# Sums over features by products with 128 moving columns, and tile 0 of a transition finished first, in a streaming-encoder trunk

## The reference, cut to what matters

```
for i in range(DEPTH):                      # DEPTH = 2
    h = modulate(rms_norm(x, norm_g[i, 0]), sh_t, sc_t)
    h = s5_mixer(...) if i % 2 == 0 else diff_attention(...)
    x = x + g_t[:, None, :] * rms_norm(h, norm_g[i, 1])
    h = modulate(rms_norm(x, norm_g[i, 2]), sh_c, sc_c)
    h = conv_ffn(h, ...)
    x = x + g_c[:, None, :] * rms_norm(h, norm_g[i, 3])
```

## Time and profile before

| what | value |
|---|---|
| time, median of 3 runs | 1262.13 us (1261.72 to 1264.94) |
| profiled execution, span from the first to the last instruction | 1260.0 us |
| PE (TensorE matmul) busy | 1216.8 us, 97% |
| DVE (VectorE) busy | 765.5 us, 61% |
| ACT (ScalarE) busy | 527.6 us, 42% |
| POOL (GpSimd) busy | 382.8 us, 30% |
| mean granted TensorE clock | 0.983 |

### The profile page before, as it was taken

One profiled execution on the slowest core, in us unless ns is written; L12 is line 12 of the kernel. 1 busy time (PEld: TensorE's weight loads), 2 busy tenths in 40 slices (PEclk: granted clock), 3 DMA queues, 4 the chain that ended last, 5 costly groups with the idle time before them and its releaser, 6 DMA issues.

```text
span 1260.0 us, 17591 instructions
## 1 busy us (share of the span) xinstructions
PE 1216.8 (97%) x6439; PEld 977.3 (78%) x6439; DVE 765.5 (61%) x1077; ACT 527.6 (42%) x809; POOL 382.8 (30%) x261
## 2 busy tenths in 40 slices
PE   5978999999999999999999999999999999999997
PEld 2757888778888887888788777678788888887886
DVE  7989587888965543242873678858744444442225
ACT  3383454244434343141432577756444443441311
POOL 4970100244654333000212443510344434331000
PEclk9989999899999999999899999998999999999999
DMA  9857645246743123223123232311132222223221
GB/s 360 305 182 210 243 159 202 98 167 225 289 165 121 67 100 125 102 93 115 46 101 117 70 99 83 90 45 67 40 127 100 85 86 96 100 100 127 83 91 67
DMA packets 26696, 162.19 MB, mean 129 GB/s; under 512 B 4496, under 2 KB 4816, under 8 KB 8400
## 3 DMA queue, kind: packets, MB, share of 16 engines
q1 hardware_dynamic: 25632, 161.15, 36.4%
q10 hardware_dynamic: 1008, 0.28, 0.1%
HBM read 152.76 MB, written 2.10 MB: 123 GB/s over the span
## 4 chain that ended last, share of the span: by engine, by line
PE 85%; DVE 8%; issue 2%; ACT 2%; DMA 1%; SPq 1%; ACTq 0%; DVEq 0%; POOL 0%
PE psum L1887 17%; PE psum L1889 17%; PE psum L1888 17%; PE psum L2001 3%; PE psum L2094 3%; PE psum L2003 3%; PE psum L2095 3%; PE psum L2096 3%; PE psum L2002 3%; PE psum L1763 2%; PE psum L2151 1%; PE psum L1952 1%; PE psum L1726 1%; PE psum L2137 1%; PE psum L2139 1%
## 5 line engine op out<-in xcount | busy, mean ns | idle before, releaser
L1887 PE MATMUL psum<-hhi,whi 128*128 128x512 f32 x960 | 378.0, 394 | 1.0 <-DVE wlo L1280 0.5
L1889 PE MATMUL psum<-hhi,wlo 128*128 128x512 f32 x960 | 374.2, 390 | 0.0
L1888 PE MATMUL psum<-hlo,whi 128*128 128x512 f32 x960 | 373.9, 389 | 0.0
L1280 DVE TENSOR_TENSOR wlo<-raw,whi 128x2048 fp32r<-128x2048 f32 x81 | 193.5, 2388 | 176.2 <-ACT whi L716 176.2
L716 ACT ACTIVATE whi<-raw 128x2048 fp32r<-128x2048 f32 x80 | 153.1, 1914 | 165.4 <-PE psum L2096 76.4
L1887 PEld LDWEIGHTS psum<-hhi,whi 128*128 128x128 f32 x960 | 180.6, 188 | 43.0 <-issue 3.5
L559 POOL TENSOR_TENSOR ca<-ca,cb 128x512 f32<-128x512 f32 x44 | 139.4, 3168 | 236.4 <-ACT ca L841 236.4
L1889 PEld LDWEIGHTS psum<-hhi,wlo 128*128 128x128 f32 x960 | 180.3, 188 | 38.1
L1888 PEld LDWEIGHTS psum<-hlo,whi 128*128 128x128 f32 x960 | 180.4, 188 | 36.0
L1445 DVE SCALAR_TENSOR_TENSOR ca<-psum,convp,ca 128x511 f32<-128x511 f32 x44 | 32.9, 748 | 204.1 <-ACT ca L837 204.1
L843 ACT ACTIVATE ghi<-ca 128x512 f32 (+1 forms) x44 | 27.8, 632 | 152.2 <-POOL ca L559 152.2
(11 more groups left out here) (366 smaller groups left out, 1854.5 us busy)
## 6 DMA issues: line engine op xcount, KB each, us to landing
raw<-in_units SPq DMA_DIRECT2D x92, 1024.0 KB, 4.8
ada_raw<-in_ada_w SPq DMA_DIRECT2D x24, 1024.0 KB, 7.4
ada_ring<-in_ada_w SPq DMA_DIRECT2D x24, 1024.0 KB, 4.8
qk_sw<-ca SPq DMA_DIRECT2D x32, 128.0 KB, 2.3
u<-in_x_blocks SPq DMA_DIRECT2D x1, 2048.0 KB, 10.4
x<-in_x_t SPq DMA_DIRECT2D x1, 2048.0 KB, 9.6
out_rows<-y_late SPq DMA_DIRECT2D x8, 256.0 KB, 2.1
bc_par<-in_s_bc SPq DMA_DIRECT2D x1, 1024.0 KB, 5.8
```

The lines of the kernel that those rows point to most:

```text
L1280: TT(wlo[:, s, :], raw[:, s, :], whi[:, s, :].bitcast(F32), ALU.subtract).then_inc(split_lo, 1)
L1887: M(out, w_hi, hi[:, k, :], start=(k == 0), stop=False)
L1888: M(out, w_hi, lo[:, k, :], start=False, stop=False)
L1889: return M(out, w_lo, hi[:, k, :], start=False, stop=(k == KT - 1))
```

## The change

All three sums now use 128 moving columns. For B the moving operand is the tile of ones. For A and C it is a table `ac_w` whose two columns are repeated 64 times: A wants weight 1 and C the squared gate, so one product of y's square gives both A (first column) and C (second column). Tiles that are summed in this way ("direct") need no second square on ScalarE and no additions for A and C on VectorE: tiles 6 and 7 in transitions 0 and 1, and all eight in transition 2, where six of them are put between the products of the last unit before the transition. The last tile's product x*g*y is no longer added to `cb[:, 0]`; TensorE takes it in from `bx`. In transition 0 it is computed from the ungated tile. The division by 1024 goes into the roots.

In `next_input` tile 0 is finished (line 1429 then 1417) before tiles 1 and 2 are gated, and `low(f)` stands behind tile f in place of tile f-1. The idle products are moved: none stands before or between the sums now, and after them 12, 5, 11 (6+2, 2, 11 in transition 2) in place of 4, 7, 14.

```diff
-        DIRECT_A, DIRECT_C = ((7,), (7,), (6, 7)), ((), (), (6, 7))
+        DIRECT = ((6, 7), (6, 7), tuple(range(KT)))
+        W_A, W_C = 3 * KT, 3 * KT + 1
...
+        def square_of(r, f):
+            if r == 2:
+                return (sq[:, 0, :], sq[:, 1, :], ca[:, 0, :], ca[:, 1, :])[f % 4]
+            return sq[:, f % 2, :] if f else ssum[:]
...
+            nc.gpsimd.memset(ac_w[:, 0:W_C, 0], 1.0).then_inc(const_ready, 1)
+            nc.gpsimd.memset(ac_w[:, W_A, 1:2], 0.0).then_inc(const_ready, 1)
+            nc.gpsimd.memset(ac_w[:, W_C, 0:1], 0.0).then_inc(const_ready, 1)
+            nc.gpsimd.memset(ac_w[:, W_C, 1:2], 1.0).then_inc(const_ready, 1)
...
 (glu_squares)
-                A(sq[:, f % 2, :] if f else ssum[:], y, ACT.Square).then_inc(sqa_ready, 1)
+                A(square_of(0, f), y, ACT.Square).then_inc(sqa_ready, 1)
                 act.wait_ge(sqa_ready, f + 1)
+                if f == KT - 1:
+                    act.wait_ge(sum_b, KT)
                 A(y, y, ACT.Copy, scale=g).then_inc(yg_ready, 1)
+                if f in DIRECT[0]:
+                    return
...
 (tile_squares)
+                if r == 2:
+                    act.wait_ge(sq_summed, 1 + (f - 3 if f >= 4 else 0))
...
 (modulation, for the first three gates)
+                            link(TT(ac_w[:, KT * i:KT * i + KT, 1], gate[:, i, :], gate[:, i, :], ALU.mult))
...
 (tile_sums)
+                ungated = r == 0 and f == KT - 1
+                if ungated:
+                    ins = STT(bx, y[:, f, :], gate[:, r, f:f + 1], x[:, f, :], ALU.mult, ALU.mult)
+                else:
+                    ins = TT(bx if f else cb[:, 0, :], x[:, f, :], y[:, f, :], ALU.mult)
+                if f in (0, KT - 1):
+                    ins.then_inc(sum_b, 1)
...
 (next_input)
                 gate_late(r, 0)
-                gate_late(r, 1)
                 dve.wait_ge(row2_psum, r + 1)
...
-                    if f + 2 < KT:
+                    if f == 0:
+                        gate_late(r, 1)
+                    elif f + 2 < KT:
                         gate_late(r, f + 2)
-                    if f:
-                        low(f - 1)
+                    low(f)
+                    if f == 0:
+                        gate_late(r, 2)
...
+            def squares_summed(tile, w, start=False):
+                for t in range(QT):
+                    ins = M(psum[:, 7, P * t:P * t + P].rearrange("p (c two) -> p c two", two=2),
+                            tile[:, P * t:P * t + P], ac_w[:, w:w + 1, :].broadcast_to([P, P // 2, 2]),
+                            start=(start and t == 0), stop=False, skip_group_check=True)
+                return ins
+            def products_summed(tile, start):
+                for t in range(QT):
+                    ins = M(psum[:, 6, P * t:P * t + P], tile[:, P * t:P * t + P], ones[:],
+                            start=(start and t == 0), stop=(not start), skip_group_check=True)
+                return ins
...
 (barrier, new)
+                if r < 2:
+                    squares_summed(ssum, W_A, True)
+                    squares_summed(cb[:, 1, :], W_C)
+                direct_squares(r, KT - 2)
+                if r != 1:
+                    products_summed(cb[:, 0, :], True)
+                direct_squares(r, KT - 1).then_inc(stat_a, 1)
+                if r == 1:
+                    products_summed(cb[:, 0, :], True)
+                products_summed(bx, False).then_inc(stat_c, 1)
+                if r == 2:
+                    idle_products(6, 0)
+                    broadcast_gate(0, 3)
+                else:
+                    idle_products(12, 0)
...
 (last unit before transition 2)
-            pe.wait_ge(sqc_ready, 2 * KT + 2)
+            pe.wait_ge(yg_ready, 2 * KT + 2)
             for step in range(2 * KT):
                 ins = gemm_step(1, step, ohi, olo, 0)
                 if step == KT - 1:
                     ins.then_inc(y_tile, 1)
+                for f in {1: (0, 1), 4: (2, 3), 11: (4, 5)}.get(step, ()):
+                    direct_squares(2, f, f == 0).then_inc(sq_summed, 1)
```

More of the change, by code:

```diff
@@ L198, in build @@
         col = sb("col", [P, 8])
+        ac_w = sb("ac_w", [P, 3 * KT + 2, 2])
         nwt = sb("nwt", [P, 4, NB])
@@ L342, in shift_col, with summed, squares_before, adds_before @@
             return layer, 24 * ffn
-        DIRECT_A, DIRECT_C = ((7,), (7,), (6, 7)), ((), (), (6, 7))
-        def sum_count(direct, r, f):
-            return sum(KT - 1 - len(d) for d in direct[:r]) + min(f, KT - 1 - len(direct[r]))
+        DIRECT = ((6, 7), (6, 7), tuple(range(KT)))
+        W_A, W_C = 3 * KT, 3 * KT + 1
+        def summed(r):
+            return KT - len(DIRECT[r])
+        def squares_before(r):
+            return sum(summed(i) for i in range(r))
+        def adds_before(r, f):
+            done = sum(max(summed(i) - 1, 0) for i in range(r))
+            return done + max(min(f, summed(r) - 1), 0)
+        def square_of(r, f):
+            if r == 2:
+                return (sq[:, 0, :], sq[:, 1, :], ca[:, 0, :], ca[:, 1, :])[f % 4]
+            return sq[:, f % 2, :] if f else ssum[:]
         POOL_CL = (5, 6, 7, 8)
@@ L807, in tile_squares @@
                 wait_y(act, r, f)
-                wait(act, sum_a, sum_count(DIRECT_A, r, f - 2) if f > 2 else 0)
-                A(sq[:, f % 2, :] if f else ssum[:], y, ACT.Square).then_inc(sqa_ready, 1)
+                if r == 2:
+                    act.wait_ge(sq_summed, 1 + (f - 3 if f >= 4 else 0))
+                else:
+                    wait(act, sum_a, adds_before(r, f - 2) if f > 2 else 0)
+                A(square_of(r, f), y, ACT.Square).then_inc(sqa_ready, 1)
                 A(y_late[:, f, :], y, ACT.Copy, scale=g).then_inc(yg_ready, 1)
-                wait(act, sum_c, sum_count(DIRECT_C, r, f - 2) if f > 2 else 0)
+                if f in DIRECT[r]:
+                    return
+                wait(act, sum_c, adds_before(r, f - 2) if f > 2 else 0)
                 A(ca[:, f % 2, :] if f else cb[:, 1, :], y, ACT.Square, scale=g).then_inc(sqc_ready, 1)
@@ L1396, in both_roots @@
                 t = nwt[:, 2, 0:QT]
-                link(TT(t, psum[:, 6, QT:2 * QT], r1, ALU.mult))
-                link(STT(t, psum[:, 6, 0:QT], 2.0, t, ALU.mult, ALU.add))
+                link(TT(t, ac[:, :, 0, 1], r1, ALU.mult))
+                link(STT(t, b[:, :, 0], 2.0, t, ALU.mult, ALU.add))
                 link(TT(t, t, r1, ALU.mult))
-                link(TT(mean, mean, t, ALU.add))
+                link(STT(mean, t, 1.0 / D, mean, ALU.mult, ALU.add))
                 rsqrt(r2, mean, 0.0, link, ALU.max)
@@ L1943, in broadcast_gate @@
                   start=True, stop=True).then_inc(mod_psum, 1)
-            def barrier(r):
[L1947 to L1951, removed]
-                        ins = M(psum[:, bank, c0 + t:c0 + t + 1], tile[:, P * t:P * t + P], col[:, 0:1],
-                                start=(start and t == 0), stop=stop, skip_group_check=True)
-                    return ins
-                pe.wait_ge(split_lo, (U_FIN[0], U_V, U_FIN[1])[r] + 1)
-                if r == 2:
-                    idle_products(5, 7)
-                pe.wait_ge(sum_a, n_a)
-                over_features(4, 0, ssum, True, False)
-                if r == 0:
-                    idle_products(4, 7)
-                for f in DIRECT_A[r]:
-                    pe.wait_ge(sqa_ready, KT * r + f + 1)
-                    ins = over_features(4, 0, sq[:, f % 2, :], False, f == KT - 1)
-                ins.then_inc(stat_a, 1)
-                if DIRECT_C[r]:
-                    pe.wait_ge(sum_c, n_c)
-                    over_features(6, QT, cb[:, 1, :], True, False)
-                    for f in DIRECT_C[r]:
-                        pe.wait_ge(sqc_ready, KT * r + f + 1)
-                        over_features(6, QT, sqc[:, f % 2, :], False, f == KT - 1)
-                pe.wait_ge(sum_b, KT * r + KT)
-                ins = over_features(6, 0, cb[:, 0, :], not DIRECT_C[r], True)
-                if not DIRECT_C[r]:
-                    pe.wait_ge(sum_c, n_c)
-                    ins = over_features(6, QT, cb[:, 1, :], False, True)
-                ins.then_inc(stat_c, 1)
-                if r == 2:
@@ L1992, in barrier @@
                   stop=True).then_inc(row2_psum, 1)
-                idle_products(14, 0 if r == 2 else 3)
+                idle_products(11, 0)
                 if r == 2:
```

47 lines of the change are left out of this document (31 added, 16 removed).

## The result

The changed kernel takes 1255.64 us (median of 5 runs, 1252.98 to 1257.38), the kernel before 1262.13 beside it (1259.7 to 1264.94): ratio 0.994, interval 0.9922 to 0.9957. It is faster, by 6.5 us of the medians. The prediction said 1257.5, from 1253.5 to 1261.5.

A forecast was written before the change was run, and what follows sets the result against it. TensorE was taken as the bound (85% of the chain), delayed at three transitions by a falling clock, idle products and VectorE. 3.05 + 0.65 + 0.95 = 4.65 off span 1260.0 gives 1255.35; median 2.1 above: 1257.5, range 1253.5 to 1261.5 us.

The forecast's parts named there:

- The clock and the price of a product: Sums at all three transitions: full clock throughout, and 0.116 us per instruction with 128 moving columns.
- the some 3 us: Estimate from the skill page, speaking against the change: wider columns would add this to each transition; the trace didn't agree.
- Transition 0: First transition: first normed tile at 235.55 in place of 239.05, 3.5 us earlier, less 0.45 for tile order; gives 3.05.
- The 0.45: Tile order at transition 0: TensorE ends 24 steps 20.5 us behind the first normed tile, before 20.05; also charged at transition 2.
- The pace: VectorE's time per tile, each low part waiting for its own tile's ScalarE copy: 2.19 us, against TensorE's 2.05.
- Transition 1: Second transition: first normed tile at 620.25 in place of 621.42, then waits for weights; gives 0.65 us.
- the waits: Transition 1: TensorE waits about 1 us for wlo before the second value unit and 0.6 before the fourth.
- Transition 2: Third transition: first normed tile at 883.85 in place of 885.27, 1.4 us earlier, less 0.45 for the order; gives 0.95.
- a change of kind: Transition 2, sums put between the last unit's products: 0.2 us for each of three, on top of 5.6 for 48 instructions.
- the full carry of the early start: Rival, chance 0.12: low parts don't hold TensorE up, gains are 4.5, 2.2 and 2.45, 9.2 in all; 1253 us.
- the worse pace: Rival, chance 0.2: each tile costs VectorE 0.25 us more, 2.44; the sum is about nothing to 1.5; 1261 us.
- The falling clock: Rival, chance 0.1: clock falls some 3.5 us into the sums despite 128 columns; first normed tiles late; 1268 us.

The follow-up runs named there:

- Narrow: The changed kernel with two and one moving columns in the sums in place of 128: 1262.88 us, ratio 0.9999 to the kernel before.
- the repeat: Kernel before, unedited, timed again: 1260.04 us, ratio 0.9976; for the attention times, the changed kernel, unedited, again: 1255.96 us, ratio 0.9945.
- wide columns alone: The kernel before with only the sums' columns widened to 128 (C in its own bank, division by 1024 in the roots): 1254.67 us, ratio 0.9942.
- Tile order of before: The changed kernel with the old tile loop in `next_input` (low part of tile f-1 behind tile f): 1255.32 us, ratio 0.9934.

## Why the prediction was right

**The clock and the price of a product** were right. The granted clock is 1.00 through all three transitions, and 40 instructions take from 219.81 to 224.28, 0.112 each against the 0.116 forecast. Narrow and wide take 1.03 and 1.05 for eight. So the some 3 us that the prediction worked out from the Trainium skill ("TensorE: Matmul & The Clock Gate", Back-to-back issue gap) did not come. That section calls its 56 ns for 128 columns an isolated gap that leaves out the loading of weights, and these products load new weights each time. Counted twice for an instruction, as the prediction counts, 56 ns is the 0.112 measured (an estimate from that section); it is the 25 ns for one column that doesn't hold here. What the same page of the Trainium skill says of the clock (The HAM clock gate), that it follows how busy the PE has been, the traces bear out only if "busy" is not the profile's busy time: 2.00 at 0.50 in one kernel, 0.95 at 1.00 in another. The cause as the prediction put it, "one-column products with gaps", was half wrong: with 128 columns the gaps did nothing.

**Transition 0**, forecast 3.05, measured 3.4 against the profile it was reckoned from and 2.7 against the repeat. The first normed tile came 3.6 earlier (3.5 forecast). The 0.45 that the prediction charged to the new order is the term that was wrong. From the first normed tile to the stage's end it is 25.57 before and 25.81 now, a loss of 0.24, and the order isn't its cause: with the order of before it is 25.86 in the changed kernel and 25.84 with wide columns alone. In the kernel before, tile 1 was gated while VectorE waited 1.10 for row 2, so GpSimd's addition was done in time; once row 2 is no longer late, normed tile 1 waits for that addition under the old order too:

```profile
237.57 0.76 DVE L1473 SCALAR_TENSOR_TENSOR psum<-x,pre_a,psum 128x512 f32<-128x512 f32 x1 [0.17 <-POOL x L572]
```

("Tile order of before", 1.51 behind tile 0's 236.06; in the kernel before it was 1.27 behind.) The pace was 2.17, not 2.19.

**Transition 1**, forecast 0.65, measured 0.9. The first normed tile moved by 1.3 (1.17). The second value unit starts 25.37 behind the sums, in place of 26.98 in the earlier trace rows; the waits are there as forecast, somewhat shorter: starts of neighbouring products lie 1.00 and 0.73 apart in place of 0.23, so 0.8 and 0.5 for forecasts of 1 and 0.6. (620.25 + 14.3 is 634.55, not the prediction's 634.65; the later wait decides, so it changes nothing.)

**Transition 2**, forecast 0.95, measured 2.0 against its own profile, 0.5 against the repeat. Here two sizes were off. The squares put between the last unit's products cost 1.70 for each 16 (852.93 less 851.23), 5.1 for all, where 5.6 plus three changes of kind at 0.2 were reckoned; a change of kind costs nothing that can be seen. And the time before isn't a fixed one: its clock had fallen within some 2.6 us of the sums' start in the profile, and only after 4.5 us in the repeat, which is worth 1.5 us and which one trace could not show.

**The sum**: 4.65 forecast, 6.3 between the two profiles, 5.2 against the mean of the two of before (170.92 - 165.73). That the median came 1.9 under the forecast is within what separates two copies of one kernel (2.9), so the closeness of the total says little, and the case rests on the stages. Of the rivals, the full carry of the early start is refuted (at transition 0 the unit starts 4.6 earlier and ends 3.4 earlier), and the worse pace too (2.17). The falling clock did not come: at sums it was seen only where the columns were narrow, where it cost 2.7, 3.2 and 1.2.

What the prediction did not ask is which parts of the change are worth having. The columns alone bring 4.9 of the 5.2 us of the stages (170.92 - 166.05), and in the runs as much as the whole (ratio 0.9942 beside 0.994 and 0.9945). The rest nets 0.3: summing so many tiles directly costs 3.1, and without that part the rest is worth 3.4 (166.05 - 162.61; 2.3 by the medians, 1254.67 and 1252.42). Finishing tile 0 first is 0.7 of that. The other 2.7 lies in parts that no run took alone: the last product from `bx`, the second squares and additions that are saved at the direct tiles left, and no idle products ahead of the sums and fewer ahead of row 2.

## What to carry to other kernels

Before you rearrange work around a reduction by thin products, look at the granted clock in stretches of it: if it falls there, widen the moving operand, which up to 128 columns cost next to nothing here (1.03 against 1.05 for eight), and measure that by itself. Then count again what is worth moving between engines with the clock steady: work taken off an engine that is waiting anyway and given to the one on the path is a loss, here 3.1 us. Take two traces of the kernel before, and compare distances within a trace and not its absolute times: 0.24% between copies of one kernel came out as if it were a difference, while the stages repeated to 0.05 us wherever the clock held.

## What was not expected of the hardware

In the first profile of the changed kernel the clock also fell in the attention, far from any sum, behind a wait of 1.58 us of TensorE. The first row is the stretch; then come the product behind the wait and two of the products in the stretch:

```profile
808.00:810.00 2.00, 2.00 (x6) 1.59 (x5) 1.90 (x6) 1.16 (x3) 0.00 (x0) 0.50 0.78 188
```

```profile
806.28 0.44 PE L2216 MATMUL psum<-ident,att 128*128 128x128 f32 x2 [1.58 <-DVE att L1645]
...
808.04 0.63 PE L1935 MATMUL psum<-olo,whi 128*128 128x512 f32 x1
808.47 0.63 PE L1936 MATMUL psum<-ohi,wlo 128*128 128x512 f32 x1
```

Products there lie 0.43 apart. From `qk_sw` to ScalarE's copy of the last unit's weights it took 171.9 in this trace, 171.0 in the repeat, 170.7 and 170.8 in the two of before, and 170.0 with wide columns alone; the table by stage leaves this out, and differences under a microsecond between kernels in the whole are no more certain than that. What makes the clock fall in one execution and not in another stays open, and so does the variation of the setup, from 219.8 to 225.5 us. One thing there goes with the kernel: both traces of the kernel before have TensorE idle for 3.4 us, up to 78.1 us, and the clock below 1.00 from 76 to 84 us, while each of the other nine has two idle stretches there, the longest of 3.36, and a clock of 1.00, "wide columns alone" too, whose code for the setup is that of before. What that is worth at the first sums isn't shown, and some of what the medians show beyond the stages (6.5 beside 5.2) may lie there. No run tried to settle any of this.
